# w_ff2 in a fused two-block float32 kernel: other 256-row pairs of a segment take the seven-product form

## The reference

```python
D_MODEL = 2048
SEQ = 256
D_FF = 4 * D_MODEL

h = rmsnorm(x, g_mlp[l])
u = jnp.square(jax.nn.relu(jnp.einsum('bsd,df->bsf', h, w_ff1[l])))
x = x + jnp.einsum('bsf,fd->bsd', u, w_ff2[l])
```

## Time and profile before

| | us |
|---|---|
| median of 3 runs | 2383.92 |
| lowest, highest | 2383.77, 2384.22 |
| profiled execution, its own time | 2383.82 |
| span of the profiled execution | 2382.0 |
| PE busy in it (12581 matmuls) | 2376.1 |
| DVE (VectorE) busy | 1700.7 |
| ACT (ScalarE) busy | 1217.8 |

### The profile page before, as it was taken

The page is one execution under the profiler, slowest core; times in us unless marked ns, Lnnn a source line. Parts: engine busy times, 40 slices in busy tenths (PEclk is TensorE's granted clock), DMA queues, the critical chain, the costliest instruction groups (busy, mean ns, idle before and its releaser), DMA issues.

```text
span 2382.0 us, 30675 instructions
## 1 busy us (share of the span) xinstructions
PE 2376.1 (100%) x12581; PEld 2034.5 (85%) x12581; DVE 1700.7 (71%) x1804; ACT 1217.8 (51%) x1427; POOL 0.2 (0%) x4
## 2 busy tenths in 40 slices
PE   9999999999999999999999999999999999999999
PEld 8888888888888888888888888888888888888887
DVE  6565666666568868868768667855778778886788
ACT  5444454554545445445445555555555455545554
POOL 0000000000000000000000000000000000000000
PEclk9999999999999999999999999999999999999999
DMA  7566556565565665655665555555555655565555
GB/s 253 160 187 196 166 186 196 191 188 196 187 186 178 219 215 186 216 182 197 200 192 189 184 185 160 170 184 186 186 182 192 201 189 174 186 219 187 187 173 181
DMA packets 238039, 452.14 MB, mean 190 GB/s; under 512 B 16569, under 2 KB 20779, under 8 KB 237771
## 3 DMA queue, kind: packets, MB, share of 16 engines
q1 hardware_dynamic: 237147, 449.07, 58.1%
q10 hardware_dynamic: 752, 1.12, 0.1%
HBM read 446.46 MB, written 3.67 MB: 189 GB/s over the span
## 4 chain that ended last, share of the span: by engine, by line
PE 97%; DVE 2%; ACT 1%; DMA 0%; issue 0%; SPq 0%; DVEq 0%; ACTq 0%
PE PS L72 97%; DVE WL L72 1%; ACT WH L72 0%; DVE PT L72 0%; DMA RAW<-in_w_in 0%; DVE TB L72 0%; DVE PB L72 0%; DVE TA L72 0%; ACT TB L72 0%; DVE TC L72 0%; DVE SEL L72 0%; DVE MHL L72 0%; ACT TA L72 0%; DVE XT L72 0%; SPq L72 0%
## 5 line engine op out<-in xcount | busy, mean ns | idle before, releaser
L72 DVE TENSOR_TENSOR WL<-RAW,WH 128x1024 fp32r<-128x1024 f32 (+1 forms) x844 | 1002.0, 1204 | 513.5 <-ACT WH L72 511.1
L72 PE MATMUL PS<-XHL,WH 128*128 128x512 f32 x3984 | 1252.7, 396 | 0.3 <-DVE XHL L72 0.3
L72 ACT ACTIVATE WH<-RAW 128x1024 fp32r<-128x1024 f32 (+1 forms) x845 | 868.9, 1043 | 736.6 <-PE PS L72 723.4
L72 PEld LDWEIGHTS PS<-XHL,WL 128*128 128x128 f32 x3968 | 745.4, 188 | 176.0
L72 PE MATMUL PS<-XHL,WL 128*128 128x256 f32 x3968 | 779.7, 278 | 0.0
L72 PE MATMUL PS<-WH,MHL 128*128 128x512 f32 x2000 | 624.0, 390 | 0.0
L72 PEld LDWEIGHTS PS<-XHL,WH 128*128 128x128 f32 x3984 | 606.6, 188 | 4.4 <-issue 0.8
L72 PEld LDWEIGHTS PS<-WH,MHL 128*128 128x128 f32 x2000 | 375.4, 188 | 77.7
L72 PE MATMUL PS<-WL,MHL 128*128 128x512 f32 x1000 | 389.1, 389 | 0.0
L72 PEld LDWEIGHTS PS<-WL,MHL 128*128 128x128 f32 x1000 | 187.8, 188 | 38.3
L72 ACT ACTIVATE MHL<-TA 128x1024 fp32r<-128x1024 f32 x33 | 35.1, 1063 | 121.7 <-DVE TA L72 121.7
(11 more groups left out here) (150 smaller groups left out, 1211.6 us busy)
## 6 DMA issues: line engine op xcount, KB each, us to landing
RAW<-in_w_ff SPq DMA_DIRECT2D x256, 512.0 KB, 4.2
RAW<-in_w_in SPq DMA_DIRECT2D x224, 512.0 KB, 3.8
RAW<-in_w_up SPq DMA_DIRECT2D x176, 512.0 KB, 4.3
RAW<-in_w_down SPq DMA_DIRECT2D x88, 512.0 KB, 4.5
RAW<-in_w_mix_out SPq DMA_DIRECT2D x32, 512.0 KB, 3.9
RAW<-in_w_out SPq DMA_DIRECT2D x32, 512.0 KB, 3.6
RAW<-in_w_conv_out SPq DMA_DIRECT2D x16, 512.0 KB, 3.5
RAW<-in_w_attn_out SPq DMA_DIRECT2D x16, 512.0 KB, 4.3
```

Source lines behind the costliest of these rows:

```text
L72: ins = step[1](*step[2], **step[3])
```

## The change

The Strassen pairs of w_ff2 are chosen by group. Group 0 uses pairs 3 and 5 (the fourth and sixth), group 1 uses pairs 1, 3 and 5. `union` lists the pairs for which left-hand sums are made, three in each segment; AXH and AXL grow to three places, and AS has no memory of its own now, but lies in SQ. The two down entries of the table name the same pairs as before for both groups.

```diff
-SEVEN = {"ff": (2, 4), "down8": (4, 5), "down6": (3,)}
+SEVEN = {"ff": ((3, 5), (1, 3, 5)), "down8": ((4, 5), (4, 5)), "down6": ((3,), (3,))}
...
-            AXH = sb("AXH", [P, 2, 4, P], f32r, c=c)
-            AXL = sb("AXL", [P, 2, 4, P], f32r, c=c)
-            AS = sb("AS", [P, 4, P], c=c)
+            AXH = sb("AXH", [P, 3, 4, P], f32r, c=c)
+            AXL = sb("AXL", [P, 3, 4, P], f32r, c=c)
             EV = sb("EV", [P, 2, 512], c=c)
-            sb("QK2pad", [P, 4096 - 1536 - 2048], c=c)
...
+        AS = SQ[:].rearrange("p (a b) -> p a b", a=4)
...
+        def union(name):
+            return sorted({n for g in SEVEN[name] for n in g})
+
-        def pairs(w, row0, kcs, col0, name):
+        def pairs(w, row0, kcs, col0, name, g):
...
-                    seven = n in SEVEN[name]
+                    seven = union(name).index(n) if n in SEVEN[name][g] else None
                     steps.append((seven, len(ents), kcs[2 * n:2 * n + 2]))
-                    if seven:
+                    if seven is not None:
...
-            sevens = [n for n, st in enumerate(steps) if st[0]]
+            sevens = [n for n, st in enumerate(steps) if st[0] is not None]
...
-                    i = sevens.index(n)
+                    i = seven
...
-            for i, pair in enumerate(SEVEN[name]):
+            for i, pair in enumerate(union(name)):
                 if pair // 2 == half_seg:
                     sums_x(i, 2 * (pair % 2), tok, after)
```

More of the change, by code:

```diff
@@ L238, in weight_order @@
                 for g in range(2 if seg < 3 else 1):
-                    pairs(io["w_ff2"][0], 2048 * seg, k16, 1024 * g, "ff")
+                    pairs(io["w_ff2"][0], 2048 * seg, k16, 1024 * g, "ff", g)
             for g in (2, 3):
@@ L258, in weight_order @@
                     pairs(io["w_down_2"][0], 512 * g0, list(range(4 * (g1 - g0))), 1024 * g,
-                          f"down{2 * (g1 - g0)}")
+                          f"down{2 * (g1 - g0)}", g)
             return len(units)
@@ L511, in group_item @@
             mid = dict(mid)
-            sevens = [n for n, st in enumerate(steps) if st[0]]
+            sevens = [n for n, st in enumerate(steps) if st[0] is not None]
             ends = [None, None]
             for n, (seven, e, kcs) in enumerate(steps):
-                if not seven:
+                if seven is None:
                     for half in range(2):
@@ L603, in sums_x @@
             v = V.step(tt, AS[:, 3, :], a12, AS[:, 1, :], sub)
-            a = A.step(act, AXH[:, seven], AS[:], AF.Copy, after=[v, ax_free.get(seven)])
-            tok[seven] = V.step(tt, AXL[:, seven], AS[:], AXH[:, seven].bitcast(f32), sub, after=[a])
+            a = A.step(act, AXH[:, seven], AS, AF.Copy, after=[v, ax_free.get(seven)])
+            tok[seven] = V.step(tt, AXL[:, seven], AS, AXH[:, seven].bitcast(f32), sub, after=[a])
         def group(w, row0, kcs, g, name):
-            steps = pairs(w, row0, kcs, 1024 * g, name)
+            steps = pairs(w, row0, kcs, 1024 * g, name, g)
             group_col[id(steps[0])] = 1024 * g
```

## The result

| | before | after |
|---|---|---|
| median of 6 runs, us | 2384.07 | 2391.88 |
| lowest and highest | 2383.77, 2385.09 | 2390.29, 2393.26 |
| ratio of the two, 95% interval | | 1.0032 [1.0021, 1.0042] |
| profiled execution, its span | 2382.0 | 2389.7 |

The change makes the kernel slower by 7.8 us, 0.33%. The prediction, 2388.4 with a range up to 2390.5, is too low.

What follows compares the result with a forecast made beforehand. PE was taken to bound the kernel; 2.04 us of saved matmuls against waits of 2.12, 2.12 and 2.31 us gave +4.5 us on the span, forecast 2388.4 us, range 2385.0 to 2390.5.

Steps and rivals of the forecast that it cites:

- the saving of nine matmuls: Group 1 of segments 0 to 2: a third Strassen pair saves three matmuls each, 2.04 us off PE.
- the walk: DVE's instruction list around group 1's start, timed from the trace: group 0's evacuation ends at T + 7.40, PE wants T + 5.44.
- T: The moment at which PE would start group 1 without a wait.
- as in w_down: A wait in w_down, used as model: the matmul stream stands as if restarted 0.16 us after DVE finished.
- 2.31 us at pair 1: Segment 1, group 1: PE's lateness, where two half sums take 1.42 in place of 1.23 us; 2.12 in segments 0 and 2.
- step 4: Last two pieces of `sevens_evac`, 2.52 us, end at T - 0.25, releasing the side group 1 wants; just in time.
- the nothing for the sums: Left-hand sums for a third pair in four segments, about 2 us of DVE each: cost nothing, 8 us at most.
- what would show it wrong: Group 1 in 41.5 us; waits at later pairs or group 1's start; granted clock under 1; changed w_ff1 or w_down stretches.
- -2.04 + 2.12 + 2.12 + 2.31 = +4.5: Whole span: nine matmuls saved, PE's lateness in group 1 of segments 0, 2 and 1 added, in us.
- the rival: Clock falls to half behind each wait for one Strassen pair: 3 x 4.76 = 14 us, 2402.7; chance 0.03.
- Longer waits by 0.1 us: Pair 1 of group 1: each wait for `group_evac` 0.1 us longer, making it slower, 2388.8 or 2389.7; chance 0.38.
- No wait: DVE reaches `group_evac` two microseconds earlier, so only the nine matmuls count: 2381.9; chance 0.10.

Runs made afterwards that it cites:

- experiment 4: The changed kernel with group 0's evacuation put two splits earlier in DVE's list, one b22 split held back: 2382.25 us, ratio 0.9992.
- Experiment 2: Against the kernel before: both groups take pairs 3 and 5, with left-hand sums of pair 1 made but unused: 2384.22 us, ratio 1.0000.
- experiment 1: The changed kernel with only two Strassen pairs in group 1, pairs 1 and 3: 2395.36 us, ratio 1.0044.
- experiment 7: The changed kernel with group 0's evacuation one split later in DVE's list, behind the split of PT: 2397.49 us, ratio 1.0054.
- experiment 5: The changed kernel with four extra matmuls on a block of zeros before the side wait in each group 1: 2389.01 us, ratio 1.0021.
- experiment 3: The changed kernel with nine extra matmuls on a block of zeros before the side wait in each group 1: 2389.46 us, ratio 1.0021.

## Why the prediction was wrong

**What held.** The bound (PE alone) and the saving of nine matmuls, 2.04 us, stand (experiment 4). So does the walk: its steps end, in segment 0 of the kernel after with T = 791.86, at T - 8.28, - 4.11, - 2.74, - 0.23, + 2.36 for PT, + 4.72 for the split of PB and + 7.43 for the evacuation, where the prediction had - 8.30, - 4.13, - 2.77, - 0.25, + 2.33, + 4.69 and + 7.40. PE restarted 0.05 us behind it, as in w_down, and group 1 takes the 43.6 us it named where the clock is full. The extra 0.19 us of segment 1 is there, but not where the prediction had it (2.31 us at pair 1): PE pays it at the start of the group, where step 4 left only 0.25 us and the restart takes 0.16 of them. Experiment 2 confirms the nothing for the sums, and no later pair waits. Of "what would show it wrong", the granted clock under 1 came true, and so did, with these 0.2 us, a wait at the start of group 1.

**The step that failed** is the sum "-2.04 + 2.12 + 2.12 + 2.31 = +4.5". It priced a stand of PE at its own length and put what the clock does behind it at nothing, with a chance of 0.03. The runs show a half clock behind two of three such stands in the profiled execution, 1.6 us each. Without a fall the time would be 2388.6 (2384.07 + 4.5), with one 2390.2, with two 2391.8. The six runs are 2390.29, 2390.82, 2391.65, 2392.10, 2392.25 and 2393.26. The mean clock is 0.999 in each, neither the 1.000 of a run without a fall nor the 0.998 of three, so each had one fall or two; these cannot be told apart by three digits, and that the lowest two runs had one is inferred from their time. The highest is 1.5 us above two falls. The kernel before also varies by over 2 us at full clock, so this need not be the clock; no run shows what it is.

**Why the chance was so wrong.** I wrote that no row shows the clock after a stand of 2 us, which was true, and then took the missing row as a reason for "no fall", while the Trainium skill (page "TensorE: Matmul & The Clock Gate", section "Loop structure matters more than you think") had the mechanism, matmuls that run at half clock behind an idle stretch. The example there is idle for 8 us; the runs here show it at 1.85 us. A cost without a row should have been bounded from both sides, with the upper end in the range. The size in the rival was off the other way: a whole Strassen pair at half clock, 4.8 us for each stand, against 1.6 measured, since only the matmuls of about 3.7 us were stretched before the clock came back.

**The other rivals.** "Longer waits by 0.1 us" did not occur. "No wait" did not either, but experiment 4 is that case, made by hand, and its price of 2.0 us below the kernel before was right.

## What to carry to other kernels

Where one engine is full, an edit that saves it work is decided by when its neighbours' in-order lists hand over what it waits for, not by how busy they are: walk the list of the releasing engine with durations from the trace, instruction by instruction, before believing an average. If the walk ends late, the first remedy is to move the releasing instructions ahead of work that is not yet due. A stand of TensorE of 2 us can cost more than its length: here the mean granted clock was below 1 in ten of the eleven runs of the two kernels that had three such stands (the kernel after and experiment 1). The page's row in tenths did not show it; the mean clock of each run and short stretches behind the wait did.

## What was not expected of the hardware

- In the one profiled execution of each kernel, the granted clock fell to half behind stands of PE of 1.84 to 1.90 us idle in two of three cases in the kernel after and three of three in experiment 1, behind stands of 3 us in two of three (experiment 7), and behind none of three of 1.0 us (experiment 5). One run of experiment 1 had no fall at all. What decides between equal stands is open; it is not their length alone.
- A fall costs 1.6 us here: in segment 0, matmuls of 512 columns start 0.43 us apart, not 0.227, for about 3.7 us.
- Nine more matmuls in each of three places made the kernel faster: 5.0 us above the kernel before instead of 7.8 (experiment 3).
